# Two chained layers on one core: the input chunks' transposes laid between the steps of the first two products

## What is computed

```python
h_res = jnp.concatenate([meta, x], axis=1)
...
for l in range(DEPTH):
    h = rmsnorm(h_res, norm_gain[l])
    proj = h @ w_in[l]
    u_pool, z_pool, c_q, c_kv, k_rope, z_mla, g_pool, g_mla = jnp.split(proj, IN_SPLIT_POINTS, axis=-1)
```

## Time and profile before

| | us |
|---|---|
| median of 3 runs | 1822.34 (1822.01 to 1823.36) |
| the profiled execution | 1825.87 |
| its span in the profile | 1823.9 |
| PE busy | 1743.3 (96%) |
| DVE, ACT, POOL busy | 1190.3 (65%), 885.2 (49%), 351.7 (19%) |
| mean granted clock of TensorE | 0.983 |

### The profile page before, as it was taken

The page is one execution under the profiler, slowest core; times in us unless marked ns, Lnnn a source line. Parts: engine busy times, 40 slices in busy tenths (PEclk is TensorE's granted clock), DMA queues, the critical chain, the costliest instruction groups (busy, mean ns, idle before and its releaser), DMA issues.

```text
span 1823.9 us, 25381 instructions
## 1 busy us (share of the span) xinstructions
PE 1743.3 (96%) x10201; PEld 1455.2 (80%) x10201; DVE 1190.3 (65%) x1686; ACT 885.2 (49%) x1394; POOL 351.7 (19%) x236
## 2 busy tenths in 40 slices
PE   8999999999999999999999999999889999999993
PEld 6998788999897677788999766766668877888882
DVE  5576644554466655555775698676774458889886
ACT  5425434234334544334344455566552356877771
POOL 3323222001243223001000375420010020000001
PEclk8999999999999999999999999999999989999997
DMA  6203112223312202322422200213145349999994
GB/s 188 76 24 99 47 47 66 97 70 116 96 59 75 70 25 69 100 93 98 143 89 93 70 24 24 70 47 115 47 138 173 116 165 391 403 403 403 404 377 173
DMA packets 158175, 245.51 MB, mean 135 GB/s; under 512 B 9625, under 2 KB 101050, under 8 KB 158058
## 3 DMA queue, kind: packets, MB, share of 16 engines
q1 hardware_dynamic: 150682, 217.07, 34.4%
q0 software_dynamic: 4464, 16.25, 2.4%
q10 hardware_dynamic: 2912, 10.55, 1.4%
HBM read 225.51 MB, written 18.35 MB: 134 GB/s over the span
## 4 chain that ended last, share of the span: by engine, by line
PE 48%; DVE 7%; ACT 4%; issue 2%; DMA 2%; POOL 0%; ACTq 0%; POOLq 0%; DVEq 0%
PE acc L1401 13%; PE acc L897 10%; PE acc L1141 8%; PE acc L1166 7%; PE acc L1230 2%; PE acc L1244 2%; PE acc L1261 1%; DVE hres L2608 1%; DMA ring<-in_w_expert_down 1%; PE acc L1252 1%; PE acc L1387 1%; DVE hres L2730 1%; DVE upad L2757 1%; DMA qk<-y_rows,back_rows 0%; PE acc L1048 0%
## 5 line engine op out<-in xcount | busy, mean ns | idle before, releaser
L897 PE MATMUL acc<-h_split,ring_split 128*128 128x264 f32 (+1 forms) x864 | 269.4, 312 | 0.0
L897 PEld LDWEIGHTS acc<-h_split,ring_split 128*128 128x128 f32 x864 | 162.3, 188 | 9.6
L1166 PE MATMUL acc<-ring_split,h_split 128*128 128x256 f32 x384 | 107.9, 281 | 0.0
L897 PE MATMUL acc<-h_split,qk_split 128*128 128x264 f32 (+1 forms) x288 | 92.7, 322 | 1.3 <-DVE ring_split L2254 1.3
L897 PE MATMUL acc<-ring_split,qk_split 128*128 128x264 f32 (+1 forms) x288 | 92.1, 320 | 0.0
L2254 DVE TENSOR_TENSOR ring_split<-ring,o_split 128x1024 fp32r<-128x1024 f32 (+1 forms) x32 | 44.9, 1417 | 64.3 <-ACT o_split L1563 64.1
L3077 POOL TENSOR_TENSOR latent<-latent 128x528 f32<-128x528 f32 x18 | 26.8, 1490 | 293.4 <-ACT latent L1558 293.0
L2254 DVE TENSOR_TENSOR ring_split<-ring,qk_split 128x1024 fp32r<-128x1024 f32 (+1 forms) x56 | 59.4, 1069 | 34.0 <-ACT qk_split L1563 34.0
L897 PE MATMUL acc<-h_split,krope_split 128*128 128x264 f32 (+1 forms) x240 | 79.4, 331 | 1.9 <-POOL ring_split L3091 1.9
L1401 PE MATMUL acc<-qk_split,krope_split 128*128 128x512 f32 x264 | 78.1, 397 | 0.0
L3091 POOL TENSOR_TENSOR ring_split<-ring,krope_split 128x1024 fp32r<-128x1024 f32 x20 | 48.1, 2406 | 152.3 <-ACT krope_split L1563 152.3
(11 more groups left out here) (598 smaller groups left out, 5608.2 us busy)
## 6 DMA issues: line engine op xcount, KB each, us to landing
ring<-in_w_in SPq DMA_DIRECT2D x64, 1024.0 KB, 5.3
ring<-in_w_expert_gate SPq DMA_DIRECT2D x10, 2048.0 KB, 15.1
ring<-in_w_expert_up SPq DMA_DIRECT2D x10, 2048.0 KB, 15.3
ring<-in_w_expert_down SPq DMA_DIRECT2D x10, 2048.0 KB, 15.6
ring<-in_w_out SPq DMA_DIRECT2D x12, 1024.0 KB, 5.2
y_rows<-gate ACTq DMA_DIRECT2D x16, 512.0 KB, 6.8
hres<-in_w_expert_up SPq DMA_DIRECT2D x3, 2048.0 KB, 15.0
qk<-in_w_expert_down SPq DMA_DIRECT2D x3, 2048.0 KB, 16.1
```

The costliest lines, as they stand in the source:

```text
L897: ins = nc.tensor.matmul(to[0:rows_], w[:, k, :], x, start=(k == 0 and i == 0), stop=(k == last and i == 2), skip_group_check=True)
L1166: ins = nc.tensor.matmul(dst[:, side, 0:WIDE], x[k][:, rows_], w, start=(k == 0 and part == 0), stop=(k == DC - 1 and part == 2), skip_gro ...
```

## The change

Four of the eight chunks are turned before the first products, as before. Chunk 4 + k is turned after step k of the two products, for k from 0 to 3, in the first layer only. Chunks 4 and 5 take accumulators; chunks 6 and 7 go to the second bank of the accumulators of 4 and 5 and join their list of readers. The copies out of PSUM read bank `c // (X_EARLY + 2)`, which is 1 for chunks 6 and 7.

```diff
+        X_EARLY = 4
...
+            def x_chunk(c):
+
+                here, n.layer = n.layer, None
+                reader = act_evacuated if c in X_BY_ACT else dve_evacuated
+                if c < X_EARLY + 2:
+                    dst = accumulator(("x", c), reader)[:, 0, :]
+                else:
+                    jobs[c - X_EARLY - 4].append((("x", c), reader, None))
+                    n.slots[("x", c), None] = n.slots[("x", c - 2), None]
+                    dst = acc[:, n.slots[("x", c), None], 1, :]
+                for i in range(4):
+                    ins = nc.tensor.transpose(dst[:, i * P:(i + 1) * P], xin[:, i, c * P:(c + 1) * P], ident)
+                done(ins, ("x", c))
+                n.layer = here
+
             def first_products():
...
                         if k == DC - 1:
                             done(ins, ("c", c))
+                    if n.layer == 0 and k < DC - X_EARLY:
+                        x_chunk(X_EARLY + k)
...
-            for c in range(DC):
-                dst = accumulator(("x", c), act_evacuated if c in X_BY_ACT else dve_evacuated)
-                for i in range(4):
-                    ins = nc.tensor.transpose(dst[:, 0, i * P:(i + 1) * P], xin[:, i, c * P:(c + 1) * P], ident)
-                done(ins, ("x", c))
+            for c in range(X_EARLY):
+                x_chunk(c)
...
-                    nc.scalar.activation(hres[:, c, META:T], acc[:, n.slot(("x", c)), 0, :], ACT.Copy)\
+                    nc.scalar.activation(hres[:, c, META:T], acc[:, n.slot(("x", c)), c // (X_EARLY + 2), :], ACT.Copy)\
...
-                    evacuated(nc.vector.tensor_copy(hres[:, c, META:T], acc[:, n.slot(("x", c)), 0, :]), ("x", c))
+                    evacuated(nc.vector.tensor_copy(hres[:, c, META:T], acc[:, n.slot(("x", c)), c // (X_EARLY + 2), :]), ("x", c))
```

## The result

| | before | after |
|---|---|---|
| median us (lowest to highest, executions) | 1823.36 (1822.01 to 1824.57, 9) | 1827.66 (1826.84 to 1830.25, 9) |
| profiled execution, us | 1825.87 | 1826.84 |
| its span, us; mean granted clock | 1823.9; 0.983 | 1824.9; 0.984 |

The ratio is 1.0026 with a 95% interval of 1.0016 to 1.0037: slower by 4.3 us. The forecast was 1828.4, with slower at 0.76. The page's busy time of PE has hardly moved (against the earlier trace rows): no work was added, PE waits elsewhere.

What follows compares the result with a forecast made beforehand. PE was taken to bound the kernel, so a start-up shift carries over: 2.9 (later squares) + 1.0 (hidden lateness and a signal) + 2.2 (half clock) = +6.1 us on 1822.34, giving 1828.4 us; range 1824.5 to 1831.3.

Steps and rivals of the forecast that it cites:

- The bound, and the shift that travels: Whole program: PE, busy 96% of the span, sets the time; a start-up shift carries through to the end unchanged.
- one of my own signs of being wrong: After 160 us: a PE wait shrinking by more than a microsecond would show the forecast wrong.
- Part 1, the early start: Start-up: first product near 16.6 us instead of 22.55, chunk 7 turned at 27.2 us instead of 19.6.
- Part 2, the later squares: ACT's squares after chunk 7: start 2.9 us later, with POOL's sum following rigidly, ending at 39.6 us.
- Part 3, the hidden 0.94 us: Before product 2: new wait for ACT's copy of `c` 0, whose 0.94 us lateness was free; gap 7.8 us, start +3.9 us.
- Part 4, the half clock: Behind the gap before product 2: PE's clock halves and costs 2.2 us, between 1.65 and 2.95.
- The sum: First 50 us: later squares, exposed lateness and half clock add to +6.1 us, carried to the end.
- the rival "+4.4 us, the clock never falls": Start-up: the clock stays full between 15 and 18 us, chunk 7 turned at 25.5 us, +4.4 us; chance 13%.

Runs made afterwards that it cites:

- experiment 7: Kernel before with one small POOL memset ahead of its weight subtraction near 1027 us: 1822.1 us, ratio 0.9989.
- Experiment 3: Changed kernel with constant matmuls filling PE's gap before product 2: 1833.32 us with 17 of them, 1828.1 us with 8.
- Experiment 1: Kernel before with one added wait, product 2 waiting for ACT's copy of `c` 0: 1825.23 us, ratio 1.0010.
- Experiment 2: Four extra unused squares on ACT ahead of its eight: 1830.31 us in the changed kernel, 1824.81 us in the kernel before.
- experiment 4: Each chunk's square moved right behind the next chunk's upper part: 1819.75 us in the changed kernel, 1825.46 us in the kernel before.
- experiment 5: Changed kernel with chunks 4 to 7 on accumulators allocated ahead of `c` 0's, so product 2 no longer takes over `c` 0's: 1826.06 us, ratio 1.0009.

## Why the prediction was right

**The bound, and the shift that travels: right.** From 50 to 1017 us every matching instruction of PE is later by the same 4.6 us (4.4 to 4.6). No slack absorbed any of it up to there. But one of my own signs of being wrong did come true: a wait of PE after 160 us shrank by more than a microsecond, the one of 1.9 us at 1027 us, and in the profiled pair it gave 2.2 us back. That was no slack, but the other outcome of a tie that I had not looked for (experiment 7).

**Part 1, the early start: right, with too long a half clock.** The first product began at 16.38 us (16.6 forecast). I let the clock fall at 18 us and rise after 3.3 us of work. It fell at 16.5 and rose at 19.9 us, so half of the spell lay ahead of the stretch that matters (18.3 us to chunk 7), and only 1.6 us of that ran at half. The transposes of a chunk cost 0.44 us (21.52 to 22.20, less 0.24 for two matmuls) where I took 0.52. Chunk 7 was turned at 26.05 and not 27.2 us. Experiment 3's 27.6 us shows that the forecast value occurs as well: this term belongs to the execution, not to the kernel.

**Part 2, the later squares: right mechanism, mis-sized term.** +1.7 us instead of +2.9. All of the 1.2 comes from chunk 7. From the squares' start to the sum's end it took 10.93 us (11.06 before), rigid as forecast, the sum itself 9.62 us.

**Part 3, the hidden 0.94 us: right.** Experiment 1 gives 1.0 for it alone. In the kernel after, 2.6 - 1.7 = 0.9. The gap was 7.65 us, forecast 7.8; both its ends came 1.1 to 1.3 us earlier than I had them. Experiment 2 shows the coupling: nothing before, at least one for one after.

**Part 4, the half clock: right.** 2.0 us (forecast 2.2, bounds 1.65 and 2.95), and 1.9 us of it disappear where PE is kept busy in the gap (experiment 3).

**The sum.** 1.7 + 0.9 + 2.0 = +4.6 us instead of +6.1; 1.2 of the 1.5 is the term of part 2. The medians differ by 4.3 us. That this is so near to 4.6 takes for granted that the tie at 1027 us came out alike in the median executions of both kernels, which no run shows; the profiled pair, where it did not, differs by 1.0. The forecast of 1828.4 was nearer to the measured 1827.66 than the sum deserves, and that is luck: I set it on the median of three runs shown, 1822.34, and the nine runs have 1823.36. I had also put the rival "+4.4 us, the clock never falls" at 13%; its sum was the nearer one, its mechanism was wrong, as the clock did fall.

**What stays open.** The 44 timings of the unchanged kernel in two of the batches of experiments fall into two groups: 29 at 1822.2 to 1823.6 and 14 at 1824.8 to 1825.9 us, with one between. 2.1 us apart is what the tie at 1027 us costs, and the four profiled executions of before and of its variants (experiments 1, 2 and 4; 1824.8 to 1826.2 us) all show the costly outcome. That the tie makes the two groups is argued, not shown: an outcome can be read only where an execution was profiled. Experiment 7 speaks in part against it, as an execution with the cheap outcome took 1824.8 us there (its shift ahead of the tie was +1.4 us). The last microsecond that the change's trace gains, behind 1035 us, goes with shorter half-clock spells there (mean clock 0.89 against 0.83 from 1490 to 1520 us), of which I haven't tested a cause.

## What to carry to other kernels

Starting TensorE earlier is worth what the next thing in line allows: follow the accumulators round the ring before moving work, and for each ask which chain frees it; a side chain that ends 0.9 us too late costs nothing until something is made to wait for it; then it costs one for one, and the clock on top. Remove limits together: here the early start alone gave +4.6 us, the early sum alone +0.2, the early start with other accumulators +2.2, with the early sum -3.9, and all of it with the clock kept up -5.5. A difference of two microseconds between two profiles has to be placed in time before it is explained, since a tie between two engines a millisecond later can give or take as much.

## What the runs showed of the hardware that I had not expected

- A 0.04 us difference in start between an operation of DVE with two inputs in SBUF and one of POOL decides over 2.1 us: 2.87 or 0.75 us for the same 128x512 operation (experiment 7). All ten traces where DVE leads have 0.75, all four where POOL leads 2.87 or 2.88.
- The clock's half spells differ between executions of like code: chunk 7 turned at 26.05 and at 27.6 us, product 2 behind a gap in 7.8 and 8.7 us, and near 580 us a spell of 3.4 us in the profile of before, of 6.8 in experiment 7 and none in experiment 4's early squares (worth 1.5 us there). Behind single gaps of 1.31 to 1.75 us the clock stood at 1.00, but it fell at 45.4 us in experiment 5, behind waits of 0.84, 1.65 and 1.14 us in six microseconds. In the gap of 7.65 us, which began at 31.90, it was at 0.50 from 36.9 us; in the one of 9.74 us, which began at 32.28, from 34.6 us.
- A matmul of 512 fp32 columns by a constant takes 0.87 us at the full clock and shows as two rows, where one of 264 columns of split operands takes 0.12.
